# The GpSimd engine's memsets among the gathers of expert rows: those of the u rows taken out

## The reference

```python
def one_block(hb):                        # 128 tokens; two such blocks
    q = (hb @ w_q).reshape(128, 8, 2, 128)                 # 8 heads
    sc = jnp.einsum('thcd,hcnd->thcn', q, sub_keys)
    s1, i1 = lax.top_k(sc[:, :, 0], 16)
    s2, i2 = lax.top_k(sc[:, :, 1], 16)
    # the 16 best of all pairs: their scores top_s and row numbers idx
    g = jax.nn.softmax(top_s, axis=-1)
    u = u_tab[idx]                        # 16 rows of 1024 a head and token
    act = jax.nn.gelu(jnp.einsum('thkd,td->thk', u, hb))
    wts = g * act
    v = v_tab[idx]                        # 16 rows of 1024 a head and token
    return jnp.einsum('thk,thkd->td', wts, v)
```

## Time and profile before

| | |
|---|---|
| median of three runs | 2458.33 us |
| the profiled execution | 2453.13 us |
| its span, first to last instruction | 2451.4 us |
| busy: TensorE matmul | 2066.6 us |
| busy: VectorE | 983.8 us |
| busy: ScalarE | 544.5 us |
| busy: GpSimd | 520.1 us |
| moved by DMA | 784.32 MB |
| of it by GpSimd's queue (gathers) | 268.47 MB |
| gathers, u and v | 256 and 256 |
| pauses, among u and among v | 64 and 64 |

### The profile page before, as it was taken

The page is one execution under the profiler, slowest core; times in us unless marked ns, Lnnn a source line. Parts: engine busy times, 40 slices in busy tenths (PEclk is TensorE's granted clock), DMA queues, the critical chain, the costliest instruction groups (busy, mean ns, idle before and its releaser), DMA issues.

```text
span 2451.4 us, 27452 instructions
## 1 busy us (share of the span) xinstructions
PE 2066.6 (84%) x8940; PEld 1172.5 (48%) x8941; DVE 983.8 (40%) x2206; ACT 544.5 (22%) x975; POOL 520.1 (21%) x688
## 2 busy tenths in 40 slices
PE   8998999667657757746799959999999999999997
PEld 7777888323223323322478854444444444444443
DVE  5854556465665675663175241111111111111113
ACT  4626201121021121011114122222222222222221
POOL 0000002566666666666000000000000000000000
PEclk9999999878778878878999979999999999999998
DMA  7352584799999999999443418699999999999995
GB/s 292 138 206 91 236 360 172 282 366 359 363 347 362 360 364 357 360 344 376 189 147 129 155 60 335 259 431 428 428 428 429 429 429 428 428 428 429 429 429 217
DMA packets 111686, 784.32 MB, mean 320 GB/s; under 512 B 13040, under 2 KB 13296, under 8 KB 80144
## 3 DMA queue, kind: packets, MB, share of 16 engines
q1 hardware_dynamic: 37904, 515.18, 50.7%
q0 software_dynamic: 73728, 268.47, 29.6%
HBM read 782.55 MB, written 1.05 MB: 320 GB/s over the span
## 4 chain that ended last, share of the span: by engine, by line
PE 47%; issue 2%; DVE 1%; DMA 1%; ACT 1%; POOL 0%; DVEq 0%; ACTq 0%; POOLq 0%
PE ps L745 42%; PE ps L904 3%; PE ps L1104 1%; DMA ring<-in_peer_v,arena 1%; PE ps L1135 0%; PE ps L1136 0%; PE ps L1061 0%; DVE arena L1800 0%; DVE ring L2051 0%; DVE arena L2053 0%; DVE ring L2052 0%; ACT arena L1339 0%; DVE arena L1803 0%; ACT arena L1411 0%; ACT arena L1416 0%
## 5 line engine op out<-in xcount | busy, mean ns | idle before, releaser
L745 PE MATMUL ps<-ring,arena 128*64 128x512 f32 (+2 forms) x3336 | 748.1, 588 | 44.2 <-issue 40.8
L904 PE MATMUL ps<-ring,arena 128*128 128x512 f32 x1024 | 484.0, 636 | 261.4 <-issue 152.3
L745 PEld LDWEIGHTS ps<-ring,arena 128*64 128x64 f32 (+1 forms) x3336 | 262.7, 140 | 502.5 <-issue 498.2
L745 PE MATMUL ps<-arena,ring 128*128 128x256 f32 x2208 | 487.8, 380 | 13.7 <-issue 8.2
L904 PEld LDWEIGHTS ps<-ring,arena 128*128 128x128 f32 x1024 | 207.7, 205 | 536.5 <-issue 529.2
L745 PEld LDWEIGHTS ps<-arena,ring 128*128 128x128 f32 x2208 | 416.5, 190 | 78.3 <-issue 15.4
L1758 DVE CUSTOM_DVE_ANT_0 ring<-ring,ps 128x1024 f32<-128x1024 f32 x256 | 312.6, 1221 | 268.2 <-DMA ring<-in_peer_u,arena 258.6
L2024 DVE TENSOR_TENSOR arena<-ps,arena 128x512 f32<-128x512 f32 x66 | 45.7, 692 | 652.8 <-PE ps L1104 652.8
L707 POOL DMA_INDIRECT ring<-in_peer_v,arena x256 | 245.3, 958 | 135.3 <-issue 108.2
L1449 ACT COPY arena<-ps 128x512 f32<-128x512 f32 (+1 forms) x198 | 108.4, 548 | 728.2 <-PE ps L745 672.1
L697 POOL DMA_INDIRECT ring<-in_peer_u,arena x256 | 240.9, 941 | 130.2 <-issue 60.8
(11 more groups left out here) (328 smaller groups left out, 1096.6 us busy)
## 6 DMA issues: line engine op xcount, KB each, us to landing
ring<-in_w_exp SPq DMA_DIRECT2D x192, 2048.0 KB, 17.1
ring<-in_w_in SPq DMA_DIRECT2D x24, 2048.0 KB, 7.9
ring<-in_w_ada SPq DMA_DIRECT2D x12, 2048.0 KB, 8.8
ring<-in_w_out SPq DMA_DIRECT2D x4, 2048.0 KB, 7.8
ring<-in_w_peer_q SPq DMA_DIRECT2D x4, 2048.0 KB, 12.1
ring<-in_w_br_rnn SPq DMA_DIRECT2D x4, 1280.0 KB, 9.3
ring<-in_w_br_attn SPq DMA_DIRECT2D x2, 2048.0 KB, 13.9
ring<-in_peer_u,arena POOLq DMA_INDIRECT x256
```

Source lines behind the costliest of these rows:

```text
L745: return pe.matmul(o, l, r, start=start, stop=stop)
L904: return pe.matmul(o, l, r, start=start, stop=False, skip_group_check=True)
```

## The change

The pause ahead of every fourth gather goes out of the loop over u rows. The one in the loop over v rows stays. `per`, the number of marks that a turn of the loop makes, falls from 84 to 76 to match.

```diff
             for tile in range(TT):
-                per = 2 * (2 + 2 * TOPK + 2 * TOPK // 4)
+                per = 2 * (2 + 2 * TOPK + TOPK // 4)
                 with pool.Fori(0, PH // 2) as i:
                     own.enter(i, per)
...
                         for k in range(TOPK):
                             if k == 4:
                                 unit_free(pool, last_in_slot(0, n_first))
-                            if k % 4 == 2:
-                                own(pool.memset(spacer, 0.0))
                             own.mark(pool.wait_ge(s_dot, i * (2 * TOPK) + TOPK * g + k + 1))
                             pool.indirect_dma_start(
```

## The result

The changed kernel takes 2487.49 us (median of 4 runs, 2484.43 to 2497.85), the kernel before beside it 2459.08 (4 runs). The ratio is 1.013, with a 95% interval of 1.011 to 1.0155: slower by 28 us, where 42 us less were forecast. The profiled execution took 2484.43 us, its span is 2482.7. In the changed kernel all lines behind 693 are two lower: u gathers are line 695, v gathers 705, dots 1756.

A forecast was written before the change was run, and what follows sets the result against it. POOL's own issue pace was taken to bound the gather stretch. 60 pauses at 0.715 us give 42.9 us, less 1.0 of lag is 41.9, so 2458.3 falls to 2416 us; range 2409 to 2434.

The forecast's parts named there:

- POOL's price: U loop: each removed pause saves POOL 0.715 us, 2.86 a group, 42.9 us over 60 pauses.
- Longer issue of the gathers: Rival: u gathers issue longer without pauses, costing 58 us, so 16 us slower, 2474 us; chance 4%.
- Transfers: Rival, gather stretch: DMA ceiling of 359 to 368 GB/s already bounds it, time 2440 to 2458 us; chance 8%.
- Dots and free buffers: Gather loops: u buffers keep 2.45 us to spare, dots take 1.22 us, v buffers stay free; none becomes a wait.
- Routes: After every second group: route is ready 3.85 us before POOL takes it; only 1.0 us of added lag comes off.
- by routes: Sign of a wrong forecast: POOL's copy idles behind the route of every second group; no size or chance given.
- Group 0: First group: gives nothing, its four pauses swallowed by POOL's wait for TensorE until 439.17 us, then some 28 us long.

The follow-up runs named there:

- e5: Kernel before with two of the four u pauses a group, v pauses as they are; 2432.73 us, ratio 0.9903.
- e13: Kernel before with each u pause replaced by five small memsets that nobody waits for; 2409.99 us, ratio 0.9812.
- e4: Kernel before, all pauses kept, with an extra 1.3 MB load by the SP queue in each of 14 groups; 2462.57 us.
- e8: Changed kernel without VectorE's best-keys search and routes in the loop, ScalarE's exponential on bounded numbers; 2377.46 us.
- e6: Kernel before with its four u pauses in one place, ahead of the third u gather; 2436.22 us, ratio 0.9925.
- e17: Changed kernel with v pauses only in even groups, plus four memsets there ahead of the fifth v gather; 2405.69 us, ratio 0.9794.
- e3: Changed kernel with each VectorE drain in search and routes replaced by a wait on its own semaphore; 2483.28 us, ratio 1.0112.
- e2: Changed kernel gathering only the first 512 of 1024 values of each row; 2429.01 us.
- e12: Changed kernel with gathers of 64 full-length rows in place of 128; 2466.06 us.
- e7: Changed kernel with four more memsets in one place, ahead of the fifth v gather; 2431.96 us, ratio 0.9902.

## Why the prediction was wrong

**POOL's price: right.** 0.715 us a pause, 2.86 a group, 16 u gathers on end in 19.96 us. e5 confirms it in time (21.1 for 21.5 us), where nothing is held up.

**Longer issue of the gathers: right to discount.** The median u gather took 0.941 us after. This rival forecast the right sign by the wrong mechanism.

**Transfers: right.** 382 GB/s at a period of 43.95 us was asked, and e13 moved 384 at a period of 43.85. The Trainium skill, "HBM Reference", section Specifications (TRN2), gives some 358 GB/s as a core's share; e13's row and e4's 385 are above it, so that rival was rightly small.

**Dots and free buffers: right where nothing is held up.** In e13 the period is 43.85 us, where the sum with its small memsets gives 44.2, and no wait of POOL for dots is longer than 0.3 us. In the changed kernel four of the five long waits for dots (15.1 of 16.9 us) follow a held-up search in the same group.

**Routes: the step that failed.** I wrote "3.85 us to spare" and "Since the v phase keeps its length, only the added lag of 1.0 us comes off". That took the 13.0 us from the last dot to the route as a constant of VectorE. It isn't one: in the changed kernel the seven routes from group 1 on take 13.0 to 26.4 us, 20.9 on average, for 12.7 to 13.6 before. That is 7.8 us more, against a cover of 3.85. The drains in them grew, and those in the search ahead of them, so that POOL's copy waits for five of the seven, up to 11.0 us. Of the 66 us of long waits, 37.6 are these; the rest are the waits for dots and for TensorE. The v phase's gathers on POOL are unchanged, and still VectorE's work beside them is slower. My last paragraph named "by routes" as a sign to look for, but no rival had it, and so neither range nor chances held it. Why VectorE's drains grow stays open, as said above.

**Group 0: wrong in the changed kernel.** "Group 0 gives nothing", but it costs 6.4 us; TensorE stands still in it for 5.4 of them and frees the ring later. In e8, with the same instructions there, it went as forecast: a wait of 27.84 us up to 439.12.

**Was there a hint?** A thin one. The drain of the kernel before has a median of 809 ns and a maximum of 2098. On chips 2 and 4 the maximum is 942, also in e6, which has as many pauses. I had read what VectorE waits for and not what its drains take.

**Where nothing is held up, the sign is the forecast one.** On chip 4, e13, which has POOL's pace of the changed kernel but for 0.07 us a place, gains 47 us (interval 38 to 54), where my sum for it would be 41.9 - 60 x 0.07 = 37.7. Whether the changed kernel itself gains there wasn't tried, so that the chip can turn the sign of this change is likely and not shown. e17, at 2405.69 us the fastest that computes all, was tried on chip 4 only.

## What to carry to other kernels

Ahead of trusting a gain in one engine's issue pace, look at the drains and the "issue" gaps of the others: a duration that varies with equal work (809 to 2098 ns) may be the sign of something that is shared, and a faster neighbour may take more of it. A cover of 3.85 us over work of 13.0 us is thin, so work out once what happens if that work takes twice as long. And time a change of this kind on more than one chip, with the changed kernel itself run again beside each group of experiments; otherwise what differs between chips or batches is read as the kernel's.

## What was new about the hardware

- VectorE's small search instructions can end 2.7 us apart while they are started 0.26 us apart (e3), with gathers on POOL beside them, and it takes neither many bytes (e2, 179 GB/s) nor all rows (e12); DMA engines that are never idle don't bring it about by themselves (e4, 385 GB/s).
- The dots, 1.22 us each, run on beside the same gathers at 1.27 us a step.
- TensorE stands still too, with nothing to wait for that the profile shows: 5.4 us in three gaps in group 0.
- The same instructions, with the same gathers beside them, took 26.4 us from the last dot to the route in one execution (the changed kernel) and 12.7 in another (e8, on chip 2).
- A memset with its wait costs POOL 0.715 us alone, but four in one place 1.58 (e7).
